# Expert layers in chunks of 32 tokens on four column tiles, gathered one chunk ahead

## The reference

```python
x = layer_norm(ALPHA * x + (1 + gate) * m, ...)          # after mixer and after experts
pg, gidx = lax.top_k(softmax(t @ w_coarse + b_coarse), 1)   # one group of four
vals, eidx = lax.top_k(softmax(fine logits of that group), 2) # two of its four experts
hid = silu(t @ w_gate[e]) * (t @ w_up[e]); out += (hid * comb) @ w_down[e]
```

## Time and profile before

| what | value |
|---|---|
| profiled execution | 934.1 us, span 931.9 us |
| PE busy | 834.0 us, 89% of the span |
| DVE, ACT, POOL busy | 40%, 27%, 11% |
| mean granted PE clock | 0.958 of full speed |
| read from memory | 277.6 MB, 302 GB/s over the span |
| gate/up products (L598) | 2176 records, 242.3 us |
| down products (L606) | 544 records, 124.2 us |
| scatters (L616) | 576 records, 83.9 us |
| gather (L578) | 192 records, 49.7 us |
| longest on the chain that ended last | loads of w_up 21%, L598 19% |

### The profile page before, as it was taken

How to read it: one execution, slowest core, us unless ns; L and a number is a source line. 1 busy time by engine, 2 the same in 40 slices (tenths; PEclk the granted TensorE clock), 3 DMA queues, 4 the chain that set the end, 5 groups by cost and what they waited for, 6 DMA issues and landing times.

```text
span 931.9 us, 15151 instructions
## 1 busy us (share of the span) xinstructions
PE 834.0 (89%) x5783; PEld 554.7 (60%) x5784; DVE 370.1 (40%) x880; ACT 248.7 (27%) x485; POOL 104.3 (11%) x148
## 2 busy tenths in 40 slices
PE   3799979998799999998989979978999998989984
PEld 2378866685695555454555558747755555555543
DVE  1159977515813332323222561266122322223253
ACT  2045682404222122122121250141222212122123
POOL 0251776000000000000000000000000000000001
PEclk9799996999899999999999979988999999999997
DMA  9996540629503999999999999393299999999701
GB/s 316 386 254 234 208 153 30 246 91 399 233 1 142 421 425 419 421 423 419 426 421 405 364 386 345 143 368 129 98 419 426 421 423 423 418 427 416 311 0 47
DMA packets 63880, 280.53 MB, mean 301 GB/s; under 512 B 3013, under 2 KB 3627, under 8 KB 55510
## 3 DMA queue, kind: packets, MB, share of 16 engines
q1 hardware_dynamic: 60738, 271.88, 73.9%
q0 software_dynamic: 2432, 6.94, 2.5%
q10 hardware_dynamic: 676, 1.24, 0.5%
HBM read 277.62 MB, written 3.37 MB: 302 GB/s over the span
## 4 chain that ended last, share of the span: by engine, by line
PE 62%; DMA 23%; DVE 7%; ACT 3%; issue 2%; SPq 1%; POOL 1%; DVEq 0%; POOLq 0%; ACTq 0%
DMA ring<-in_w_up 21%; PE bank L598 19%; PE bank L850 6%; PE bank L606 6%; PE bank L578 5%; PE bank L616 4%; PE bank L472 4%; PE bank L711 4%; DMA ring<-in_w_ada 2%; DVE t L1190 2%; PE bank L505 2%; PE bank L514 2%; PE bank L491 1%; PE bank L543 1%; PE bank L906 1%
## 5 line engine op out<-in xcount | busy, mean ns | idle before, releaser
L598 PE MATMUL bank<-ring,work 128*64 128x256 f32 x2176 | 242.3, 380 | 26.5 <-DMA ring<-in_w_up 25.5
L598 PEld LDWEIGHTS bank<-ring,work 128*64 128x64 f32 x2176 | 171.3, 137 | 94.6 <-issue 38.4
L1649 DVE TENSOR_TENSOR acc<-acc,bank 128x528 f32<-128x528 f32 x144 | 95.0, 701 | 125.1 <-PE bank L616 125.1
L606 PE MATMUL bank<-ring,work 128*64 128x512 f32 x544 | 124.2, 599 | 0.0
L1642 DVE TENSOR_TENSOR work<-work,bank 128x128 f32<-128x128 f32 x68 | 19.6, 288 | 214.3 <-ACT work L1126 123.7
L616 PE MATMUL bank<-work 64*128 64x264 f32 x576 | 83.9, 409 | 3.6 <-DVE work L1663 2.9
L616 PEld LDWEIGHTS bank<-work 64*128 64x128 f32 x576 | 49.4, 186 | 41.5 <-issue 31.3
L711 PE MATMUL bank<-h,ring 128*128 128x264 f32 x320 | 73.9, 390 | 0.0
L606 PEld LDWEIGHTS bank<-ring,work 128*64 128x64 f32 x544 | 36.0, 136 | 62.3 <-issue 58.2
L1806 POOL COPY work<-work 128x512 f32 x32 | 19.7, 615 | 422.1 <-PE bank L598 422.1
L711 PEld LDWEIGHTS bank<-h,ring 128*128 128x128 f32 x320 | 60.0, 190 | 11.5 <-issue 0.8
(11 more groups left out here) (247 smaller groups left out, 842.5 us busy)
## 6 DMA issues: line engine op xcount, KB each, us to landing
ring<-in_w_gate SPq DMA_DIRECT2D x32, 2048.0 KB, 17.3
ring<-in_w_up SPq DMA_DIRECT2D x32, 2048.0 KB, 21.2
ring<-in_w_down SPq DMA_DIRECT2D x32, 2048.0 KB, 21.8
ring<-in_w_ada SPq DMA_DIRECT2D x24, 2048.0 KB, 19.8
ring<-in_w_in_even SPq DMA_DIRECT2D x5, 2048.0 KB, 33.0
ring<-in_w_out_even SPq DMA_DIRECT2D x2, 2048.0 KB, 10.0
ring<-in_w_out_odd SPq DMA_DIRECT2D x2, 2048.0 KB, 21.0
con<-in_shape_constants SPq DMA_DIRECT2D x1, 1078.0 KB, 16.9
```

Of the source, the lines that this page charges most:

```text
L598: last = mm(GU[j][r, 0:2 * P].rearrange("p (a n) -> p a n", a=2), hgc[:, k, :], ring[:, s:s + 2, c0:c0 + P], start=(k == 0), stop=(k == KD ...
L606: last = mm(Y[C * dh:C * (dh + 1), :], hidt[:, j, C * hf:C * (hf + 1)], wd[:, 2 * hf + j, 512 * dh:512 * (dh + 1)], start=(j == 0 and hf = ...
L1649: v.tensor_tensor(acc[:, q:KD:4, :], acc[:, q:KD:4, :], banks[:, 4 + 2 * (q % 2):6 + 2 * (q % 2), 0:T], ALU.add).then_inc(m["added_" + "ab ...
```

## The change

- A chunk has 32 rows instead of 64. Gate/up, down and the gather run on four column tiles of 32 columns instead of two of 64, the scatter on four row tiles of 32 rows instead of two of 64. A chunk holds all of its columns in one bank, so there is one sigmoid and one pair of DVE products for it.
- There is no gather of all rows. The rows of a chunk have their slots at a multiple of 32; POOL makes the one-hot matrix of the next chunk (picks), PE gathers it behind gate/up (12 products of 256 columns, tokens on partitions), ACT copies, PE turns it with two transposes, ACT copies again to hgc.
- The SwiGLU result is turned by sixteen products of 32 columns with a part of the identity, which take every fourth column, so that the down matrix is read with each partition's 16 KB in one piece; it is loaded so.
- DVE adds a scattered chunk times the gate straight into x, in two halves of four banks, and the eight samples to a small sum. The residual after the experts is then done, and the layer norm sums x.
- The routing places the rows once instead of twice, counts chunks with one comparison and one sum, and no longer makes the start of each chunk. The clearing moves ahead of the layer norm. ACT writes htm in another order of its columns.
- In the attention ACT copies the values ahead of the exponential, and ten taps instead of five stand behind it.

The core of the diff (added lines that belong together; the rest is names, constants and what falls away):

```diff
-C = 64
-WIDE = 96
-HS = 2 * T
-HGW = HS + C
+C = 32
 
 MAXCH = EXPERTS + (2 * T) // C + 1
+STEPS = (T + C - 1) // C
 ALPHA = (2 * 2) ** 0.25
...
-                return w.rearrange("(k p) n -> p k n" if i == 2 else "(p k) n -> p k n", p=P)
+                return w.rearrange("(p k) n -> p k n", p=P)
...
+                def gather(n):
+
+                    pe.wait_ge(m["picked"], n)
+                    for t in range(TT):
+                        k = min(P, T - t * P)
+                        for q in range(4):
+                            last = mm(GATH[C * q:C * (q + 1), :], pk[0:k, t, :], htm[0:k, t, 2 * P * q:2 * P * (q + 1)],
+                                      start=(t == 0), stop=(t == TT - 1), tile_position=(0, C * q))
+                    last.then_inc(m["gathered"], 1)
+
+                def turn(n):
+
+                    pe.wait_ge(m["gath_copied"], n)
+                    for b in range(2):
+                        last = tr(TURN[:, P * b:P * (b + 1)], gath[:, P * b:P * (b + 1)], ident)
+                    last.then_inc(m["turned"], 1)
...
+                def gate_up(s, ks):
+
+                    for k in ks:
+                        for q in range(4):
+                            c0 = FF * k + P * q
+                            last = mm(GU[C * q:C * (q + 1), :].rearrange("p (a n) -> p a n", a=2),
+                                      hgc[:, P * (k % 2) + C * (k // 2):P * (k % 2) + C * (k // 2 + 1)],
+                                      ring[:, s:s + 2, c0:c0 + P], start=(k == 0), stop=(k == KD - 1),
+                                      tile_position=(0, C * q))
                     return last
 
+                def down(wd):
+
+                    for q in range(4):
+                        for dq in range(4):
+                            last = mm(Y[C * dq:C * (dq + 1), :], hidt[:, C * q:C * (q + 1)],
+                                      wd[:, q, 2 * P * dq:2 * P * (dq + 1)], start=(q == 0), stop=(q == 3),
+                                      tile_position=(0, C * dq))
+                    last.then_inc(m["down_done"], 1)
+
+                def scatter(b, n):
+
+                    pe.wait_ge(m["added_" + "ab"[b]], n)
+                    if b:
+                        pe.wait_ge(m["added_a"], pe.snap(n + 1))
+                    for dq in range(4):
+                        r = slice(C * dq, C * (dq + 1))
+                        last = mm(bank[4 + dq][:, 0:T], ysb[r, P * b:P * (b + 1)], sct[r, :], start=True, stop=True,
+                                  tile_position=(C * dq, 0))
+                    last.then_inc(m["scattered_" + "ab"[b]], 1)
...
                         with pe.Fori(lo, hi) as g:
-                            g1 = pe.snap(g + 1)
-                            a1, a2 = pe.snap(2 * g + 1), pe.snap(2 * g + 2)
+                            g1, g2 = pe.snap(g + 1), pe.snap(g + 2)
                             pe.wait_ge(m["chunk_ready"], g1)
                             for i in range(2):
                                 pe.wait_ge(unit_in[(u + i) % RING], filled[i])
-                            gate_up(0, s, m["gu1_done"])
-                            gate_up(1, s, m["gu2_done"])
-                            pe.wait_ge(m["hid1_done"], g1)
-                            tr(HT[:, 0:P], hid[:, 0, :], ident).then_inc(m["ht1_done"], 1)
+                            gate_up(s, range(4))
                             pe.wait_ge(m["y_copied"], g1)
                             pe.wait_ge(m["scat_ready"], g1)
-                            scatter(0, m["added_a"], a1)
-                            scatter(1, m["added_b"], a1)
-                            pe.wait_ge(m["hid2_done"], g1)
-                            pe.wait_ge(m["ht1_copied"], g1)
-                            tr(HT[:, P:2 * P], hid[:, 1, :], ident).then_inc(m["ht2_done"], 1)
+                            scatter(0, g1)
+                            gate_up(s, range(4, KD)).then_inc(m["gu_done"], 1)
+                            gather(g2)
+                            pe.wait_ge(m["hid_done"], g1)
+                            for k in range(KF):
+                                for q in range(4):
+                                    r = slice(C * q, C * (q + 1))
+                                    last = mm(HT[r, C * k:C * (k + 1)], hid.rearrange("p (i k) -> p k i", k=KF)[:, k],
+                                              ident[:, r], start=True, stop=True, tile_position=(0, C * q))
+                            last.then_inc(m["ht_done"], 1)
+                            scatter(1, g1)
+                            pe.wait_ge(m["ht_copied"], g1)
+                            turn(g2)
                             pe.wait_ge(unit_in[(u + 2) % RING], filled[2])
-                            down(0, wd)
-                            pe.wait_ge(m["ht2_copied"], g1)
-                            down(1, wd).then_inc(m["down_done"], 1)
-                            scatter(2, m["added_a"], a2)
-                            scatter(3, m["added_b"], a2)
+                            down(wd)
...
-                if s >= 4:
+                if 4 <= s <= LEVELS:
                     taps(10 * (s - 4) + 5, 10 * (s - 3))
-            act.wait_ge(E("kl_diff"), 1)
-            A(fn(dE[:, 0:2 * SEQ], dE[:, 0:2 * SEQ], ACT.Exp), E("kl_exp"))
             z_tile(22)
             for tt in range(2):
                 act.wait_ge(*attended(f"v_tr{tt}"))
                 copy(vtm[:, tt, :], bank[2 + tt][:, :], E("vtm_copied"))
             act.wait_ge(*attended("vs_tr"))
             copy(vstm[0:NS, :], bank[7][0:NS, :], E("vs_copied"))
-            taps(50, 55)
+            act.wait_ge(E("kl_diff"), 1)
+            A(fn(dE[:, 0:2 * SEQ], dE[:, 0:2 * SEQ], ACT.Exp), E("kl_exp"))
+            taps(45, 55)
...
+                act.wait_ge(m["gathered"], 1)
+                copy(gath, GATH, m["gath_copied"])
+                act.wait_ge(m["turned"], 1)
+                copy(hgc, TURN, m["chunk_ready"])
                 act.wait_ge(m["table_ready"], l + 1)
                 total = act.value_load(tab[l][0:1, EXPERTS:EXPERTS + 1], min_val=EXPERTS, max_val=MAXCH)
                 with act.Fori(0, total) as g:
+                    g1, g2 = act.snap(g + 1), act.snap(g + 2)
+                    act.wait_ge(m["gu_done"], g1)
+                    fn(sig, GU[:, 0:P], ACT.Sigmoid).then_inc(m["sig_done"], 1)
+                    act.wait_ge(m["gathered"], g2)
+                    fn(gath, GATH, ACT.Copy).then_inc(m["gath_copied"], 1)
+                    act.wait_ge(m["ht_done"], g1)
+                    fn(hidt, HT, ACT.Copy).then_inc(m["ht_copied"], 1)
+                    act.wait_ge(m["turned"], g2)
+                    fn(hgc, TURN, ACT.Copy).then_inc(m["chunk_ready"], 1)
                     act.wait_ge(m["down_done"], g1)
+                    act.wait_ge(m["scattered_b"], g1)
...
+                tt(over, count.unsqueeze(2).broadcast_to([P, EXPERTS, STEPS]),
+                   con[:, K_NCH:K_NCH + STEPS].unsqueeze(1).broadcast_to([P, EXPERTS, STEPS]), ALU.is_gt)
+                S.sync()
+                S(v.tensor_reduce(nch, over, AX_X, ALU.add))
                 S.sync()
                 S(v.tensor_tensor_scan(incl, onef[:, :], nch, 0.0, ALU.mult, ALU.add))
+                S.sync()
+                tt(cbase, incl, nch, ALU.subtract)
+                S.sync()
+                stt(rank2, cbase.unsqueeze(1).broadcast_to([P, TT, EXPERTS]), float(C), ranks, ALU.mult, ALU.add)
                 S.sync()
                 tt(prods, pick2, rank2.unsqueeze(1).broadcast_to([P, 2, TT, EXPERTS]), ALU.mult)
                 S.sync()
+                S(v.tensor_reduce(pslot, prods, AX_X, ALU.add))
+                S.sync()
+                tt(past, pslot.unsqueeze(3).broadcast_to([P, 2, TT, NCH + 1]),
+                   wide4(con[:, K_BASE:K_BASE + NCH + 1], NCH + 1), ALU.is_ge)
+                S.sync()
+                S(v.tensor_reduce(psum_c, past, AX_X, ALU.add))
+                tt(hot_b, past[:, :, :, 0:NCH], past[:, :, :, 1:NCH + 1], ALU.subtract)
+                S.sync(1)
+                stt(pslot, psum_c, -float(C), pslot, ALU.mult, ALU.add)
+                S.sync()
+                tt(hot_r, wide4(con[:, K_SLOT:K_SLOT + C], C), pslot.unsqueeze(3).broadcast_to([P, 2, TT, C]),
+                   ALU.is_equal, E("picks_ready"))
...
+                def add_all(b, g1):
+                    added, scattered = (m[n + "_" + "ab"[b]] for n in ("added", "scattered"))
+                    dve.wait_ge(added, g1)
+                    dve.wait_ge(scattered, g1)
+                    v.tensor_tensor(sacc[:, b], sacc[:, b], banks[:, 4:8, SEQ:T], ALU.add)
+                    for dq in range(4):
+                        i = 2 * dq + b
+                        last = v.scalar_tensor_tensor(out=x[:, i, 0:SEQ], in0=bank[4 + dq][:, 0:SEQ],
+                                                      scalar=gate[:, i, 0:1], in1=x[:, i, 0:SEQ], op0=ALU.mult, op1=ALU.add)
```

(19 more changed lines are left out.)

310 lines of the change are left out of this document (98 added, 212 removed).

## The result

The changed kernel takes 935.1 us (median of 20 runs, 928.59 to 940.8), the kernel before 930.2 us (20 runs, 927.88 to 933.89): 1.005 times as long, 95% interval 1.0035 to 1.0064. The forecast was 925.4 us, faster by 0.5%, with a range of 907 to 951. The time lies in the range, the sign was wrong. The profiled execution of the changed kernel took 932.9 us.

What follows compares the result with a forecast made beforehand. Expert layers, half the span, were bound by TensorE first, then by weights. +41.1 (chunks) - 39.0 (ahead) - 0.8 (behind) - 6.5 (attention) = -5.2 us: 934.1 to 928.9, less 3.5 for the median, 925.4 us; range 907 to 951.

Steps and rivals of the forecast that it cites:

- Behind them, -0.8: Last chunk's end to the end of the sums: 9.75 and 8.45 us instead of 9.9, less 0.7 for late modulation weights.
- The chunk, 9.1 us: Expert layers: a 32-token chunk takes 9.1 us of TensorE, ends 8.8 and 10.6, instead of 13.34 for 64 tokens.
- Rival A: Expert chunks: the sixteen products' loads don't overlap, chunk 10.0 us, in all +21.5, 952 us; chance 0.28.
- C: Expert loops: instructions are fetched again as the loop bodies grow, gaps of 3 us or more per pair; chance 0.08.
- New expert, 0.85 and 1.4: Start of a new expert: 0.85 or 1.4 us come free on the path where TensorE bounds, nothing where weights are awaited.
- The recurrence: Expert layers, modelled by chunk ends and weight arrivals: 263.6 and 257.9 us, together 521.5 against 480.4, +41.1 us.
- The weights: Expert layers: weight matrices land one after another, 4.98 us each instead of 5.03, with 16 KB blocks.
- Ahead of the chunks, -39.0: Front of both layers: first product 19.7 us earlier in each, less 0.25 for the slower clock; ends -36 and -42.
- Attention, -6.5: Attention, values copied ahead of the exponential: 5.0 us of wait and 1.5 of slower clock saved; ends -8 and 0.
- The 3.5 us taken off: Whole kernel: the median of 930.6 us lies 3.5 below the profiled 934.1, so 928.9 became 925.4.
- 2.0 and 1.7 us: Expert layers, slow clock: 2.0 us added to a chunk after a wait for weights, 1.7 to a layer's first chunk.

Runs made afterwards that it cites:

- half_down: Changed kernel, loading only half of each expert's down matrix, the rest of the slot holding old data: 914.8 us, 0.9839 of the kernel before.
- busy_front: Changed kernel with nine unused TensorE products ahead of each layer's first gather and four behind the tables: 927.1 us, 0.9978 of the kernel before.
- busy_tail: Changed kernel with three unused TensorE products between a layer's two last scatters and three behind them: 935.7 us, 1.0054 of the kernel before.
- one_turn: Changed kernel with one 128x128 turn for the sixteen products, down matrix in 4 KB rows again: 926.8 us, 0.9973 of the kernel before.

## Why the prediction was wrong

The forecast difference was -5.2 us, the measured one is +4.9. No single step turned the sign; several were priced too low, one of them above all. Against the table's forecast row the two profiles of the changed kernel are, on average, 2.8 us shorter in the opening and 0.9 in the attention, but 2.3 us longer in the two fronts, 3.4 in the two layers and 5.1 behind the layers. So from the first front to the end 10.8 us were missed.

**The step that failed is the term "Behind them, -0.8"**: it stood for 3.1 us less than before on the table's cuts, and the changed kernel has 2.0 us more there. The front's gather and tables, put at the full clock, come next, then the chunk, 0.1 us too short 49 times.

- **The chunk, 9.1 us**: right, 9.19. The sixteen products were put at 0.65 and take 0.62. Rival A is ruled out by it, and C by the gaps and by 24 packets on the instruction queue, where the earlier trace rows has 23. The 0.1 us is worth 2.5 to 2.9 us by the prediction's own rule, and layers 0 and 1 are 0.7 and 2.6 us longer than forecast, 3.4 together. It is small in the chunk and not in the sum.
- **New expert, 0.85 and 1.4**: right, 0.8 and 1.3.
- **The recurrence**: right, but for the chunk that it was fed with. It gave 263.6 and 257.9 us; the means are 264.3 and 260.5, and half_down's layer 0 came out within 1 us.
- **The weights**, 4.98 us a matrix: 4.89, better, and worth no more than that.
- **Ahead of the chunks, -39.0**: -36.7 (12.9 and 12.7 us against 30.9 and 31.4). The ranks' chain, 3.55 us, was right (3.6). The tables were put at 0.7 us and take 2.06, the gather at 1.7 and takes 2.94. Both run at the 1.2 GHz level behind 4.8 us of idle PE; in busy_front, at the full clock, they take 1.32 and 1.64. So the gather was mis-sized by the clock alone, the tables half by the clock and half by themselves. The prediction had 0.25 us for the slow clock in the fronts, and 1.7 for a layer's first chunk, which is 2.4 longer than the next (11.60 against 9.19).
- **Behind them, -0.8**: the step that failed most. On the table's cuts it forecast 115.8 and 30.5 us; the means are 118.3 and 33.1, 5.1 us more. From the last down product to the end of the sums it forecast 9.75 and 8.45 us; the two traces have 11.2 and 11.2 in layer 0, 10.3 and 11.5 in layer 1, where the kernel before has 11.0 each: nothing was gained. The scatters wait 2.0 us for DVE's add, as forecast, but what follows runs slowly: in layer 1 the sums (5.51 and 6.39 us, before 3.83), in layer 0 the modulation's products ahead of them (L471 in the first line below, 3.08 us, where 32 such records take 1.94 at the full clock). And the modulation's weights come late (the second line): 13.5 and 13.1 us from the sums to the transposes of the pooling layer, before 11.3, so 1.7 to 2.1 us, put at 0.7. The slow products are a matter of the clock, which busy_tail shows for layer 1; the late weights no run tested.

```profile
512.54 3.08 PE L471 MATMUL bank<-ring,cT 128*32 128x256 f32 x32
...
529.95 1.29 PE L471 MATMUL bank<-ring,cT 128*32 128x256 f32 x20 [2.09 <-DMA ring<-in_w_ada]
```

- **Attention, -6.5**: right within what can be told: 6.0 us between the means of ten and four traces, 5.3 to 6.35 on the kernel before, 3.0 (0 to 6) on the changed one. The value copies' wait is gone, the products behind them start with no idle time, against 5.10 us in the earlier trace rows:

```profile
130.66 1.08 PE L778 MATMUL bank<-acc,con 8*64 8x256 f32 x8
```

- **The 3.5 us taken off** to come to the median: right in kind. That execution took 934.1 us, more than any of the 20 timed ones. Its opening was 2.0 to 2.2 us and its stretch between the layers 2.6 us longer than in two others, with a lower granted clock each time (0.74 against 0.87 from 20 to 46 us; 0.86 against 1.00 in the windows above). The opening's part is gone in the changed kernel too (42.4 and 43.0 us against the forecast's 45.5). The part between the layers is not: from the transposes of the pooling layer to the ranks its two profiles have 93.2 and 94.6 us, as the slow trace of before (94.0) and not as the other two (91.5).

The steps that fell short have one thing in common but for the chunk and the late weights. The change takes long, dense work off TensorE (the gather of 24.6 us, chunks of twice the rows) and leaves short work between waits; the durations that I took for it came from stretches at full clock. The mean granted clock was 0.958 to 0.965 in the three profiles of before and 0.942 and 0.931 in those of after. TensorE was busy at the 0.50 clock for 57.5, 47.6 and 52.3 us in those of before, 81.7 and 102.4 us in those of after. If such work takes twice its time, as the gather nearly does (2.94 against 1.64 us), the low clock costs 20 us more than before, an estimate from these sums. The layers have most of it (25 and 13 to 17 us, before none), and there the forecast had counted it with its 2.0 and 1.7 us; in each front it is 5.6 us (before 3.0 to 4.2), in the end 8.4 and 11.3 us (before 4.9), and there it had not.

With TensorE kept busy in the fronts the time is 927.1 us. That it lies within 1.7 us of the forecast is luck: the stages behind the layers (117.2 and 32.3 us) are still above the forecast's, and the profiled execution of that kernel took 930.8 us. What stays open is the share of the stages behind the layers by time: busy_tail mends the end in its trace and not its median, and no run loads the modulation's weights earlier.

The Trainium skill (TensorE: Matmul & The Clock Gate, Part 1) says that how many products run at the low clock when a kernel warms up differs between its runs, and calls the penalty of that ramp under 1% of a typical span. The traces agree on the first. Here the clock falls again and again: half of the 82 to 102 us, an estimate as above, is 4 to 5% of the span. The extra products in the fronts gave back 6.7 to 8.0 of 935.1 us, 0.7 to 0.9%, more than the whole forecast difference of 0.5%.

## What to carry to other kernels

Where an edit replaces long products by short ones between waits, price what follows a wait at the clock that the trace grants behind such waits, not at the full one. A few unused products in the wait show whether that is the cause, and may be the cure. Price also the small error of a step that runs 49 times. And take the difference between two kernels only after seeing one stage in several executions: here the same instructions differed by 4 us.

## What the hardware showed unexpectedly

- A moving operand read every fourth float (16 bytes apart) takes twice the time: 3.80 us instead of 1.91 for 32 records of 256 columns, 1060 us instead of 927 in all (one_turn, where they are packed).
- Sixteen products of 32 columns on four column tiles take 0.62 us, against 0.26 for the one turn of 128x128 that they replace.
- Where the clock falls differs between executions of one kernel, and the time follows: in the stretch to the ranks TensorE was busy at the 0.50 clock for 9.9 and 10.1 us in the two traces that took 188.2 us, and for 21.8 to 22.2 us in the five that took 192.1 to 192.3, with the same instructions.
- 16 KB blocks instead of 4 KB rows bring 0.23 us for 2.1 MB (14.68 against 14.91 us for three matrices).
